# Three rearrangements in a three-block transformer kernel: state-space vectors and two z projections moved, latent keys put into a feed-forward part, the latent mixer written as one stage

## What is computed

```
# block 1, second half (one layer), x: (256, 1024)
ckr    = rms_norm(x, kv_in_norm) @ w_dkv                 # 256 latent + 64 rope columns
c_kv   = rms_norm(ckr[:, :256], kv_lat_norm)
k_rope = rope(ckr[:, 256:]);  k_nope, v = split(c_kv @ w_ukv)   # 6 heads x (128 + 128)
x      = x + 0.5 * swiglu(rms_norm(x, ffn1_norm), ffn1_w_gu, ffn1_w_down)
cq, q_mem = split(rms_norm(x, mix_norm) @ b_w_in)        # 256 + 256 columns
q      = rms_norm(cq, b_q_norm) @ b_w_uq                 # 6 heads x (128 + 64), the 64 through rope
o_b    = softmax(mask(q . k) * 192**-0.5) @ v            # 6 heads
o_m    = softmax(q_mem . mem_k * 64**-0.5) @ mem_v       # 4 heads of 64
x      = x + concat(o_b, o_m) @ w_out
# block 2, hybrid mixer: attention, then a Mamba-2 branch
z, xbc, dt = parts of h @ w_in_2;  xbc = silu(causal_conv(xbc))
dt = softplus(dt + dt_bias);  a = -exp(a_log)
y  = ssd_scan(x, dt, a, B, C) + d_skip * x;   y = rms(y * silu(z)) * norm_w;  then gates and projections
```

## Time and profile before

| | |
|---|---|
| median of 3 runs | 3173.77 us (3173.66 to 3181.37) |
| the profiled execution, its own time | 3177.92 us |
| its span in the profile | 3176.1 us |
| PE busy | 2925.6 us (92%) |
| DVE / ACT busy | 1825.2 / 1467.7 us |
| mean granted TensorE clock | 0.947 of 2.4 GHz |

### The profile page before, as it was taken

One profiled execution on the slowest core, in us unless ns is written; L12 is line 12 of the kernel. 1 busy time (PEld: TensorE's weight loads), 2 busy tenths in 40 slices (PEclk: granted clock), 3 DMA queues, 4 the chain that ended last, 5 costly groups with the idle time before them and its releaser, 6 DMA issues. The chain is left out here.

```text
span 3176.1 us, 47818 instructions
## 1 busy us (share of the span) xinstructions
PE 2925.6 (92%) x20616; PEld 2713.9 (85%) x20616; DVE 1825.2 (57%) x2468; ACT 1467.7 (46%) x1954; POOL 16.3 (1%) x21
## 2 busy tenths in 40 slices
PE   6998788997997899999998899999997899998899
PEld 6998686996897599899998798998997799997798
DVE  4567464654554565645458756556553665655655
ACT  4454213543544354443557454444454454544543
POOL 0000000000000000000000100000000000000000
PEclk9998786998999799999999999999998899999899
DMA  6655100663564055555536255554555356563564
GB/s 193 192 179 160 54 1 27 190 195 97 171 192 137 20 187 193 178 187 185 161 115 188 63 167 168 191 186 159 187 183 162 120 187 192 178 190 129 175 191 133
DMA packets 371974, 489.29 MB, mean 154 GB/s; under 512 B 17119, under 2 KB 331060, under 8 KB 371636
## 3 DMA queue, kind: packets, MB, share of 16 engines
q1 hardware_dynamic: 371168, 486.03, 48.1%
q10 hardware_dynamic: 596, 0.21, 0.0%
HBM read 485.14 MB, written 1.05 MB: 153 GB/s over the span
## 5 line engine op out<-in xcount | busy, mean ns | idle before, releaser
L839 PE MATMUL work<-input_hi,weights_hi 128*128 128x256 f32 x3520 | 989.3, 281 | 15.0 <-PEq L151 6.8
L841 PE MATMUL work<-input_lo,weights_hi 128*128 128x256 f32 x3520 | 985.9, 280 | 0.0
L842 PE MATMUL work<-input_hi,weights_lo 128*128 128x256 f32 x3520 | 985.8, 280 | 0.0
L224 DVE TENSOR_TENSOR weights_lo<-weights_raw,weights_hi 128x2048 fp32r<-128x2048 f32 (+2 forms) x282 | 629.3, 2235 | 433.7 <-ACT weights_hi L207 433.6
L839 PEld LDWEIGHTS work<-input_hi,weights_hi 128*128 128x128 f32 x3520 | 666.6, 189 | 20.3 <-DVE weights_lo L229 13.5
L841 PEld LDWEIGHTS work<-input_lo,weights_hi 128*128 128x128 f32 x3520 | 666.7, 189 | 3.7
L842 PEld LDWEIGHTS work<-input_hi,weights_lo 128*128 128x128 f32 x3520 | 666.3, 189 | 0.0
L211 ACT ACTIVATE weights_hi<-weights_raw,params 128x512 fp32r<-128x512 f32 (+1 forms) x736 | 462.1, 701 | 372.4 <-DMA weights_raw<-in_ffn_w_in 180.3
L229 DVE SCALAR_TENSOR_TENSOR weights_lo<-weights_raw,params,weights_hi 128x512 fp32r<-128x512 f32 (+1 forms) x736 | 492.7, 731 | 212.3 <-ACT weights_hi L211 212.2
L207 ACT ACTIVATE weights_hi<-weights_raw 128x2048 fp32r<-128x2048 f32 (+2 forms) x282 | 524.9, 1864 | 187.5 <-DMA weights_raw<-in_ffn_w_up 107.2
L314 PE MATMUL acc<-weights_hi,hidden_hi 128*128 128x512 f32 x880 | 345.3, 392 | 5.5 <-DVE hidden_lo L922 5.4
(11 more groups left out here) (468 smaller groups left out, 3250.0 us busy)
## 6 DMA issues: line engine op xcount, KB each, us to landing
weights_raw<-in_ffn_w_gu SPq DMA_DIRECT2D x176, 512.0 KB, 4.8
weights_raw<-in_ffn_w_in SPq DMA_DIRECT2D x176, 512.0 KB, 4.7
weights_raw<-in_ffn_w_down SPq DMA_DIRECT2D x66, 1024.0 KB, 4.9
weights_raw<-in_w_in SPq DMA_DIRECT2D x44, 1024.0 KB, 5.3
weights_raw<-in_ffn_w_out SPq DMA_DIRECT2D x44, 1024.0 KB, 5.0
weights_raw<-in_a_w_in SPq DMA_DIRECT2D x29, 1024.0 KB, 5.5
weights_raw<-in_ffn_w_gate SPq DMA_DIRECT2D x44, 512.0 KB, 3.9
weights_raw<-in_ffn_w_up SPq DMA_DIRECT2D x44, 512.0 KB, 5.0
```

Source lines behind the costliest of these rows:

```text
L224: last = self.nc.vector.tensor_tensor(self.wl[:, n % SLOTS, 0:kc * cols], raw, self.wh[:, n % SLOTS, 0:kc * cols].bitcast(F32), ALU.subtract)
L839: nc.tensor.matmul(o, wh[:, k, ms], K.hi[:, c, :], start=(c == 0 and m == 0), stop=False, skip_group_check=True)
L841: nc.tensor.matmul(o, wh[:, k, ms], K.lo[:, c, :], start=False, stop=False, skip_group_check=True)
L842: last = nc.tensor.matmul(o, wl[:, k, ms], K.hi[:, c, :], start=False, stop=(c == DC - 1), skip_group_check=True)
```

## The change

1. **Vectors.** `a_log_2`, `dt_bias_2` and `d_skip_2` are fetched at the start of the kernel, as whole rows spread over the partitions, into a lasting `head_rows`. `hybrid_conv`'s SP has no wait and no loads of vectors; DVE copies the two halves of `d_skip` out of the row.
2. **z items.** The first two of the eight z items are projected at the end of `hybrid_conv`, behind its 16 items; their silu goes to `zt`, and `state_space` waits for it. `hybrid_gates` has 18 items instead of 20 and on PE waits for the state space before its first projection. Some buffers share memory (`cbm`, `xdec`, `dtT`).
3. **Latent keys.** `latent_keys`, `rope_tables` and `rotate` go. Class `LatentKeys` does the same work in steps 0 to 4 of the feed-forward part that follows; `plan_ffn` has its 5 items behind the a and b items of steps 0 and 1. `ffn` follows the one before without a barrier.
4. **Latent mixer.** One joined stage with 8 items holds the two projections, the norm, the query heads, ten heads of attention and the output product, with the four memory heads first. The order of `w_out`'s items is changed to match.

The core of the diff, with the engines' orders that the text speaks of:

```diff
 def plan_ffn(K, gate, up, g0, u0, down, gain, between=None):
...
+        if between:
+            between(s)
...
@@ start, sync
+            for i, row in enumerate((A["a_log_2"], A["dt_bias_2"], A["d_skip_2"])):
+                sp.dma_start(K.head_rows[:, i, :], row.rearrange("(a h) -> a h", a=1).to_broadcast([P, SH]))\
+                    .then_inc(*K.constants_loaded.up(16))
@@ ffn, tensor
+                    if keys and s == 1:
+                        keys.sum_squares(pe)
                     K.arrived(pe, b_item(s))
...
+                    if keys and s == 0:
+                        keys.project(pe, b_item(s) + 1)
+                    if keys and s == 1:
+                        keys.expand(pe, b_item(s) + 1)
@@ LatentKeys, scalar
+    def take(self, act, n):
...
+        for i in range(NH // 2):
+            K.round_weights(act, n + i + 1 + LEAD)
+            act.wait_ge(K.used, n + i + 1)
+            nc.scalar.activation(K.k_nope[:, 2 * i:2 * i + 2, :], K.acc[:, 2 * (i % 2), :].rearrange("p (j t) -> p j t", j=2),
+                                 ACT.Copy).then_inc(*self.passed.up())
...
@@ latent_mixer, tensor
+                for h in range(MH, HEADS):
+                    for i, q in (((0, 0), (0, 1)), ((0, 2), (0, 3)), (), ((1, 0),), ((1, 1), (1, 2)), ((1, 3),))[h - MH]:
+                        if (i, q) == (1, 0):
+                            pe.wait_ge(*split(MH + 2))
+                        out_quarter(i, q)
+                    turn(h)
+                    if h + 2 < HEADS:
+                        scores(h + 2)
+                    if h > MH:
+                        mix(h - 1)
+                mix(HEADS - 1)
@@ latent_mixer, scalar
+                for h in range(MH, HEADS):
+                    K.round_weights(act, OI + 3 + h - MH)
+                    take(h)
+                    if h > MH:
+                        attended(h - 1)
+                    if h + 2 < HEADS:
+                        exps(h + 2)
@@ latent_mixer, vector
+                for h in range(MH, HEADS):
+                    divide(h)
+                    if h + 2 < HEADS:
+                        soften(h + 2)
+                    if h > MH:
+                        attended(h - 1)
+                    K.split_weights(dve, OI + 3 + h - MH)
@@ hybrid_conv
-        with K.stage(ITEMS, join=True) as (block, n0):
+        with K.stage(ITEMS + 2, join=True) as (block, n0):
             @block.sync
             def _(sp):
-                sp.wait_ge(*before)
-                for i, row in enumerate((A["a_log_2"], A["dt_bias_2"])):
...
+                for i in range(2):
+                    act.wait_ge(K.used, n0 + ITEMS + i + 1)
+                    nc.scalar.activation(zt[:, i, :, :], K.work[:, i, :].rearrange("p (m t) -> p m t", m=2), ACT.Silu)\
+                        .then_inc(*opened.up())
@@ hybrid_gates, tensor
+                pe.wait_ge(*before)
+                for i in range(2, 12):
...
@@ state_space, tensor and scalar
+                pe.wait_ge(*done)
...
+                act.wait_ge(*done)
@@ build
-            latent_keys(K, latent)
...
-            ffn(K, latent, FeedTail(K, mix), join=False)
-            latent_mixer(K, mix)
-            project_out(K, K.h, DC, FeedTail(K, second))
+            ffn(K, latent, FeedTail(K, mix), keys=keys)
+            latent_mixer(K, mix, FeedTail(K, second))
```

More of the change, by code:

```diff
@@ L669, in await_row, with plan_ffn @@
         pass
[L672 removed]
+def plan_ffn(K, gate, up, g0, u0, down, gain, between=None):
     for s in range(NF):
@@ new lines, in turn @@
+                def turn(h):
+                    pe.wait_ge(*normed(2 * h + 2))
+                    if h:
+                        pe.wait_ge(*taken(h))
+                    for t in range(NT):
+                        for kt in range(NT):
+                            last = nc.tensor.transpose(K.work[:, 2, kt * T + t * P:kt * T + (t + 1) * P],
+                                                       p_[:, h % 2, t, kt * P:(kt + 1) * P], K.c("ident"))
+                    last.then_inc(*turned.up())
@@ new lines, in mix @@
+                def mix(h):
+                    pe.wait_ge(*taken(h + 1))
+                    if h:
+                        pe.wait_ge(*split(h))
+                    for kt in range(NT):
+                        v = K.mem_v[:, 1, kt, h * MD:(h + 1) * MD] if h < MH else K.v_mla[:, kt, (h - MH) * P:(h - MH + 1) * P]
+                        last = nc.tensor.matmul(K.work[rows(h), 3, 0:T], v, pT[:, h % 2, kt, :], start=(kt == 0), stop=(kt == NT - 1))
+                    last.then_inc(*mixed.up())
@@ new lines, in swap, with out_quarter @@
+                def swap(x, bank):
+                    for j in range(x.shape[1]):
+                        last = nc.tensor.matmul(K.acc[0:ROPE, bank, j * T:(j + 1) * T], K.c("swap")[0:ROPE, :], x[:, j, :],
+                                                start=True, stop=True)
+                    last.then_inc(*swapped.up())
+                def out_quarter(i, q):
+                    if q == 0:
+                        K.arrived(pe, OI + i)
+                    last = K.quarter(pe, OI + i, pair(i), BY_TOKENS[q], i == 0, False)
+                    if q == 3:
+                        last.then_inc(K.used, 1)
@@ new lines, in _ @@
+                K.project(pe, n0, K.work[:, 0, :], (K.hi, K.lo), lambda k: feed.before_chunk(pe, k))
+                feed.sum_row(pe)
+                K.project_part(pe, n0 + 1, K.work[:, 1, :], (K.hi, K.lo), 0)
+                pe.wait_ge(*squared(1))
+                for c in range(2):
+                    last = nc.tensor.matmul(K.work[:, 2, 0:T], K.c("ones"), sq[:, c, :], start=(c == 0), stop=(c == 1))
+                last.then_inc(*summed.up())
+                K.project_part(pe, n0 + 1, K.work[:, 1, :], (K.hi, K.lo), 1)
```

632 lines of the change are left out of this document (410 added, 222 removed).

## The result

The changed kernel takes 3133.45 us (median; 3131.04 to 3136.45) against 3174.57 us for the kernel before (3173.66 to 3181.37). The ratio is 0.9861, with a 95% interval of 0.9849 to 0.9873. It is faster by 41 us where 67 were forecast, and it lies 3 us above the upper end of the range. The profiled execution took 3136.45 us for a span of 3134.7.

The account below looks back on a forecast made before the run. PE, busy 92% of 3176.1 us, sets the pace, so only stretches where it does not stream can shrink. Savings of 34 + 13 + 12 + 8.4 = 67.4 from 3177.92, less 4.15, give 3106 us; range 3088 to 3130.

Parts of the forecast that it names:

- The woven work: Latent-key products moved into the feed-forward part, where PE has no idle time, counted in full: 22.7 us added.
- The norm's chain: Latent keys, step 1: from the sum to the end 5.5 us, just fitting beside the b item's 5.6 us.
- the wait behind the expansion: End of the latent keys: PE waits some 1.2 us for ACT's last copy before gate products may write the same banks.
- F: Feed-forward part: each of the five woven items waits half a landing, 12 us in all, giving 3118; chance 4%.
- G: Feed-forward part: the ring's lead is lost, eleven steps cost 337 us more, giving 3443; chance 2%.
- the memory heads: Latent mixer: the four heads placed first, done at about 39 us from the start of the stretch.
- the last quarter of the second item: Latent mixer: the second output item's last quarter, after six heads of one round each, ends at 78.3 us.
- the turn behind the wait: Latent mixer: after 11.25 us for landing, rounding, split and division of the next part's third item, at 89.55 us.
- the clock's term: Latent mixer: loss to the half clock behind waits, 5 us, making 110.5 us from 105.5.
- Three waits of over 4 us remain in my order: Latent mixer: each followed by about 4.6 us at half speed, costing 2.3 us; 5 us in all.
- the circle's sum: Latent mixer round: turn, score, masking, low half, split and division in sequence, 8.0 us, or 8.7 with a gain item.
- rival D: The whole latent mixer runs at the half clock, 25 us more, giving 3131; chance 5%.

Follow-up runs that it names:

- padding 128: Changed kernel with 128 bytes of unused buffer behind the lasting vector rows, against the kernel before: 3121.40 us, ratio 0.9819.
- the second profile: The kernel before, unedited, run and profiled once more: 3176.67 us, ratio 0.9995.
- padding 256: Changed kernel with 256 bytes of unused buffer, hidden halves at 0 modulo 512, against the kernel before: 3133.96 us, ratio 0.9865.
- padding 384: Changed kernel with 384 bytes of unused buffer, hidden halves at 128 modulo 512, against the kernel before: 3117.29 us, ratio 0.9814.
- Filler in the waits: Three unused constant matmuls ahead of the turn in five mixer rounds: changed kernel 3126.97 us; with padding, early split and later item too, 3099.79 us.
- The early split: Changed kernel with DVE's weight split put behind the division, ahead of the masking, in the mixer's rounds: 3127.59 us, ratio 0.9837 to the kernel before.
- the later item: Changed kernel with the next feed-forward part's third item rounded and split behind the last attended head: 3118.71 us, ratio 0.9813 to the kernel before.

## Why the prediction was wrong

**Part 3, the latent keys: what was added is right, what was removed was 4.3 us too long.** The woven work was put at 22.7 us; with the padding it is 22.9 (384.4 us, less the 361.5 of the two parts without the removed stretch). 34 us were forecast; against the first profile of before the trace gives 29.7, and 33.6 with the padding (384.4 us against 418.0). Against the second profile (413.3) these are 25.0 and 28.9. The sum took the stretch of 56.50 us from one execution, in which it ran at 0.68 of the clock; in three other profiles it takes 52.2 to 52.9. And the sum then took off 4.15 us more because that execution was slower than the median. The two profiles differ by 4.9 us in all (3176.1 and 3171.2) and by 4.3 in this stretch, so about 4 us of the forecast were counted twice. The norm's chain fitted beside the b item, the wait behind the expansion was 1.18 us for 1.2, and no item was late (rivals F and G fall).

**Parts 1 and 2, the hybrid mixer: right.** 12 us for the vectors are measured alone. The z items take 11.2 us; the state space begins 12.7 us behind the convolution's last item and not 9.5, so 3.2 us and not 1.8 are lost there; the gates and outputs give 9.6 us (78.6 to 69.0) where 10.2 stood. In all 20.2 for 20.4, or 18.1 against the second profile of before (472.4 us).

**Part 4, the mixer: the mechanism was right, its size was not.** 13 us were forecast, 6.0 came. Step by step from 971.9, where the prediction puts its zero: the memory heads end at 40.9 (39 in the sum), the last quarter of the second item at 86.2 (78.3), the turn behind the wait at 98.9 (89.55), the mixer at 117.7 (105.5 without the clock's term). So the memory heads are 1.9 us over the sum, the rounds 6.0, the wait 1.4 and what follows it 2.9, in all 12.2 us, where the sum had 5 for the clock. The step that failed is "Three waits of over 4 us remain in my order, each with about 4.6 us at half speed behind it": of waits that long there was one, and the half clock lasted for 20 us in the rounds (0.50 from 1027 to 1047), behind a wait of 1.63 us and through one of 3.86, and again from 1061 to 1078, during and behind the long wait. Four rounds took 37.8 us where 8.0 to 8.7 each are 33. A score at the half clock is 4.6 us (4 x 1.15) and at the full one 2.5. With 12.2 us for 5, 7.2 us are missing in the sum.

That the clock lengthens the rounds, and by how much, is shown by the four kernels whose mixer is the same code and which differ in padding alone. Rounds of heads 4 to 7, us, each with its granted clock:

| run | head 4 | head 5 | head 6 | head 7 |
|---|---|---|---|---|
| changed kernel | 7.54 at 1.00 | 9.64 at 0.60 | 11.72 at 0.50 | 8.87 at 0.94 |
| padding 128 | 7.54 at 1.00 | 7.94 at 1.00 | 11.68 at 0.50 | 11.72 at 0.62 |
| padding 256 | 7.54 at 1.00 | 7.93 at 0.88 | 11.73 at 0.50 | 8.40 at 0.99 |
| padding 384 | 7.54 at 1.00 | 10.08 at 0.57 | 11.73 at 0.50 | 8.38 at 1.00 |

The views of head 5's round in the changed kernel and with 128 bytes, and of head 7's with 128 and 384 bytes:

```profile
1024.99:1034.63 9.64, 5.78 (x17) 2.96 (x17) 4.86 (x8) 4.41 (x10) 0.00 (x0) 0.60 0.31 104
1021.15:1029.09 7.94, 4.04 (x17) 2.26 (x17) 4.76 (x8) 4.25 (x10) 0.00 (x0) 1.00 0.36 122
1040.77:1052.49 11.72, 10.94 (x28) 6.89 (x28) 5.31 (x11) 1.96 (x6) 0.00 (x0) 0.62 0.00 0
1039.80:1048.18 8.38, 6.82 (x28) 4.51 (x29) 5.21 (x11) 2.08 (x6) 0.00 (x0) 1.00 0.00 0
```

At or near the full clock the rounds are 7.5, 7.9 and 8.4 us, as the circle's sum of 8.0 to 8.7 has them; at the half clock the same rounds take 1.7 to 3.3 us more. Head 6's round ran at the half clock in all four. My ground for the step, the rate of the clock loss after one wait of 4.78 us, was one row carried to a place of another kind, where short waits follow one another. The Trainium skill, "TensorE: Matmul & The Clock Gate", section "HAM oscillation — how this bites in real kernels", warns of just such bursts between waits. This trace agrees in part: 0.80 for the mixer and 0.75 to 0.77 in the rounds; but not each burst ran at the low clock, since head 4's round had 1.00. I gave this a chance of its own (rival D), but only as the whole mixer at the half clock, for 25 us, where a part of it was, for about 7.

How much of it belongs to the edit is less certain than the figures look. The mixer's code is the same in the changed kernel and in the three padded ones, and it took

| run | mixer, us | granted clock |
|---|---|---|
| changed kernel | 138.5 | 0.83 |
| padding 128 | 138.1 | 0.85 |
| padding 256 | 141.1 | 0.81 |
| padding 384 | 134.6 | 0.86 |

from the end of the last gate product to the next one. The time goes with the clock, and both differ between programs whose code here is the same; the kernel before has 0.80 in both of its profiles. Filler in the waits did not pay. In one run the clock of the rounds was 0.77, which the kernel with 256 bytes of padding has without filler; in the other it was 0.95 and not 0.80, but the rounds were longer by about the filler's own time in one of them. The early split and the later item, which shorten the waits, bring the clock from 0.83 to 0.93 and, with the padding, the mixer to 115.4 us. What makes the clock fall in one round and not in the next is not shown; idle PE alone is not what keeps it down.

**What the sum did not have: 12 us for placement.** "Sum. 34 + 13 + 12 + 8.4" has only terms for instructions that the change adds, removes or moves. The 384 bytes of `head_rows` slow 2640 matmuls that are not touched, by 5 ns each: 2640 x 0.005 = 13 us, measured 12 by the padding. That is the largest part of the 26 us that are missing; the mixer's clock and wait are 7, and the stretch that was counted too long is 4. The rest is about 3 us, and I do not put it down to any part of the change: the second feed-forward part begins at 558.4 in the first profile of before and between 557.9 and 566.1 in the profiles of the eleven experiments, and the median of the kernel before lies between 3174.57 and 3177.84 us in the four sets of runs.

With placement as before and nothing else, the changed kernel stands at 3121 us, inside the range that I gave. The range holds the 15 us that then remain to 3106; it does not foretell what they are made of.

## What to carry to other kernels

A buffer that is added early moves all that are allotted behind it. Before and after such an edit, compare the mean time of instructions that were not touched, and try one or two paddings: here 128 bytes were worth 12 us, as much as any of the four rearrangements but one. When work is woven into a streaming part, count it in full and count the chain beside it: 22.7 us were forecast and 22.9 measured. Take a stretch that is to be removed from more than one profile: here one execution had 56.5 us for it and three had 52.2 to 52.9. When a ring of buffers couples two stages, look for the first item that can be fetched only when the present stage has used its last but one: no engine may have to treat it ahead of its own urgent work.

## What the runs showed of the hardware

- Matmuls with 512 moving columns start 227 ns apart when the stationary operand (hidden) lies 0 or 256 bytes, modulo 512, from the moving one (weights), and 232 ns apart at 128 or 384; four placements of the changed kernel and two of the kernel before agree. The weights stood at 128 in all of them, so distance and place of the stationary operand are not told apart. Why is not shown.
- The clock fell to its half level in rounds whose longest waits were 1.63 and 3.86 us. With three matmuls more per round the rounds ran at 0.77 in one kernel (0.71 to 0.77 in four without them) and at 0.95 in another (0.80 without, one profile each); in neither were they shorter by more than 0.1 us.
- PE stayed at the half clock through 13.6 us without idle time in one profile, and through 27.1 us with 25.48 busy in another.
- The same round of the same code took 7.94 us at the full clock and 10.08 at 0.57, another 8.38 at 1.00 and 11.72 at 0.62.
- Behind a table load of 1.28 us the next activation began 0.02 us later.
